# Token sums moved from GpSimd to ScalarE and VectorE, and six weight tiles split once for both token sides, in a decoder trunk on one core

## What is computed

```python
def _adaln(x, gain, mod, j):
    n = _rms(x.astype(jnp.float32)) * gain
    return (n * (1.0 + mod[:, 3 * j + 1]) + mod[:, 3 * j]).astype(x.dtype)

def _swiglu(h, w_gate, w_up, w_down):
    return (jax.nn.silu(h @ w_gate) * (h @ w_up)) @ w_down
```

## Time and profile before

| | us |
|---|---|
| median of three executions | 2867.88 |
| the three | 2866.21, 2867.88, 2873.26 |
| the profiled execution | 2879.42 |
| its span, first to last instruction | 2877.7 |
| TensorE busy in it | 2642.8 (92%) |
| mean granted TensorE clock | 0.942 |

### The profile page before, as it was taken

One profiled execution on the slowest core, in us unless ns is written; L12 is line 12 of the kernel. 1 busy time (PEld: TensorE's weight loads), 2 busy tenths in 40 slices (PEclk: granted clock), 3 DMA queues, 4 the chain that ended last, 5 costly groups with the idle time before them and its releaser, 6 DMA issues. The chain is left out here.

```text
span 2877.7 us, 52261 instructions
## 1 busy us (share of the span) xinstructions
PE 2642.8 (92%) x22580; PEld 2461.4 (86%) x22580; DVE 1719.4 (60%) x2353; ACT 1047.2 (36%) x1484; POOL 775.2 (27%) x530
## 2 busy tenths in 40 slices
PE   3999999999689998899999899999999498899998
PEld 0999988899378876899998899998889378799998
DVE  2868725743466645788852687852632356877824
ACT  2444414322533322444432434442421433444523
POOL 2665201000011021365510156610000121456301
PEclk7999999999689988999999999999999589999999
DMA  6222455721100013332245432255651113322324
GB/s 247 74 89 96 145 182 163 250 85 46 57 2 3 3 55 128 118 103 96 95 169 172 130 103 96 92 173 169 217 187 52 50 20 132 109 92 94 100 81 127
DMA packets 82349, 316.74 MB, mean 110 GB/s; under 512 B 9400, under 2 KB 14408, under 8 KB 80584
## 3 DMA queue, kind: packets, MB, share of 16 engines
q1 hardware_dynamic: 82120, 313.40, 32.7%
HBM read 302.63 MB, written 10.74 MB: 109 GB/s over the span
## 5 line engine op out<-in xcount | busy, mean ns | idle before, releaser
L165 DVE TENSOR_TENSOR weights_r<-work,weights_r 128x1024 fp32r<-128x1024 f32 (+2 forms) x318 | 436.5, 1373 | 356.8 <-ACT weights_r L161 356.5
L161 ACT ACTIVATE weights_r<-work 128x1024 fp32r<-128x1024 f32 (+2 forms) x318 | 313.1, 985 | 584.5 <-PE banks L860 341.8
L756 POOL TENSOR_TENSOR rows<-rows,consts 128x288 f32<-128x288 f32 (+3 forms) x64 | 88.4, 1381 | 691.5 <-ACT consts L967 691.5
L858 PE MATMUL banks<-low_r,weights_r 128*128 128x288 f32 (+2 forms) x1112 | 270.1, 299 | 0.0
L856 PE MATMUL banks<-h_r,weights_r 128*128 128x288 f32 (+1 forms) x904 | 226.0, 305 | 42.0 <-DVE big_r L419 25.8
L858 PE MATMUL banks<-big_r,weights_r 128*128 128x288 f32 (+2 forms) x960 | 244.1, 299 | 0.0
L856 PE MATMUL banks<-low_r,weights_r 128*128 128x288 f32 (+2 forms) x832 | 215.5, 306 | 27.1 <-DVE weights_r L165 18.3
L773 PE MATMUL banks<-h_r,weights_r 128*128 128x288 f32 x788 | 233.1, 296 | 1.6 <-DVE weights_r L165 0.8
L774 PE MATMUL banks<-big_r,weights_r 128*128 128x288 f32 x788 | 232.3, 295 | 0.0
L775 PE MATMUL banks<-h_r,weights_r 128*128 128x288 f32 x788 | 232.1, 295 | 0.0
L860 PE MATMUL banks<-h_r,weights_r 128*128 128x288 f32 (+1 forms) x904 | 221.5, 300 | 0.0
(11 more groups left out here) (550 smaller groups left out, 7079.1 us busy)
## 6 DMA issues: line engine op xcount, KB each, us to landing
work<-w_ff_dram SPq DMA_DIRECT2D x130, 512.0 KB, 3.7
h<-w_mod_dram SPq DMA_DIRECT2D x48, 768.0 KB, 5.3
work<-w_down_dram SPq DMA_DIRECT2D x66, 512.0 KB, 3.5
consts<-w_ff_dram SPq DMA_DIRECT2D x64, 512.0 KB, 3.6
work<-w_mod_dram SPq DMA_DIRECT2D x32, 768.0 KB, 9.1
work<-w_in_even_dram SPq DMA_DIRECT2D x24, 512.0 KB, 3.7
big_buf<-w_mod_dram SPq DMA_DIRECT2D x16, 768.0 KB, 6.0
consts<-w_down_dram SPq DMA_DIRECT2D x22, 512.0 KB, 3.6
```

The costliest lines, as they stand in the source:

```text
L161: return act.activation(high, raw, ACT.Copy)
L165: return engine.tensor_tensor(low, raw, high.bitcast(F32), ALU.subtract)
L756: pool.tensor_tensor(k.rows[:, c], k.rows[:, c], k.square[:, c], ALU.add).then_inc(added, 1)
L858: pe.matmul(out[a], high[:, w], x[a][1], start=False, stop=False)
```

## The change

It has three parts.

1. **Six tiles split once.** In U2 to U4 the side 1 units take the split tiles of side 0 (`add_again`; a `Piece` with `raw` None does nothing on ScalarE and VectorE and has no load). p3, p4 and p5 go to three extra places in `low_r`, which are free once the stage before has ended. p0 to p2 keep the three usual places. So 18 loads, 18 high splits and 18 low splits are gone.
2. **Token sums by VectorE.** L278 is gone: ScalarE adds the shift in place to the scaled tokens that are still there (`shift`, 16 small activations in a stage), and the four sums are made by VectorE (`mix`). GpSimd keeps the weight sums alone.
3. **One more plain unit in U1.** `PLAIN` is 3, so the scheme begins at the fourth unit there. The PSUM pairs of the scheme are rotated by two for it.

```diff
-PLAIN_SKEWED, PLAIN = 4, 2
+PLAIN_SKEWED, PLAIN = 4, 3
...
-    def mix(self, pool, mixed):
-
-
-        norm, n = self.norm, self.sums
-        for a in range(2):
-            pool.wait_ge(norm.low_done[a], KT + a)
-            pool.tensor_tensor(norm.temp[a], norm.high[a].bitcast(F32), norm.low[a].bitcast(F32), ALU.add)\
-                .then_inc(mixed, 1)
...
+    def shift(self, act, a, kt, shifted):
+
+        width = self.norm.prompt[a + 1] - self.norm.prompt[a]
+        at = self.norm.temp[a][:, kt, 0:width]
+        act.activation(at, at, ACT.Identity, bias=self.norm.mod[:, kt, 0:1]).then_inc(shifted, 1)
+
+    def mix(self, dve, name, shifted, mixed):
+        done = self.split + self.order.index(name)
+        if name == "t3":
+            dve.wait_ge(shifted, 2 * KT * (self.number + 1))
+            one, other, op = self.b22, self.b12, ALU.subtract
...
+        dve.tensor_tensor(one, one, other, op).then_inc(mixed, 1)
...
+        def add_again(u, earlier):
+            for i, lo, hi in earlier.pieces:
+                last_use[pieces[i].place] = len(pieces)
+                u.pieces.append((len(pieces), lo, hi))
+                pieces.append(Piece(u, None, None, pieces[i].place, None, pieces[i].nth_split))
...
+            if number:
+                begins = [stage.side_first(a) + 1 + part for a in range(2) for part in range(2)]
+                mixes, highs, lows = (f - 5, f - 4, f - 3, f - 2), (f - 2, f - 2, f - 1, f + 1), (f - 2, f - 1, f - 1, f + 1)
+            else:
+                begins = [f - 6, f - 6, f - 5, f - 5]
+                mixes, highs, lows = (f - 4, f - 3, f - 2, f - 1), (f - 4, f - 3, f - 2, f + 1), (f - 3, f - 2, f - 1, f + 1)
...
                     if stage.kind == "up":
                         if number:
                             pool.wait_ge(piece_done, stage.first)
-                        mixing[stage].mix(pool, tokens_mixed)
...
-                    if i >= SPLIT:
-                        act.wait_ge(piece_done, i - SPLIT + 1)
...
+                    if piece.free_behind >= 0:
+                        act.wait_ge(piece_done, piece.free_behind + 1)
...
+                    for scheme, a, part in shift_at.get(i, ()):
+                        act.wait_ge(scheme.norm.low_done[a], KT + a)
+                        for kt in range(part * KT // 2, (part + 1) * KT // 2):
+                            scheme.shift(act, a, kt, tokens_shifted)
+                    for scheme, name in high_at.get(i, ()):
+                        mixed_high(scheme, name)
```

More of the change, by code:

```diff
@@ L261, in __init__ @@
         self.k, self.stage, self.norm = k, stage, norm
-        self.sums, self.split = 6 * number, 4 * number
+        self.number, self.split = number, 4 * number
+        rotated = 2 * ((PLAIN_SKEWED if norm.after else PLAIN) % 2)
+        self.pairs = [(b + rotated) % 4 for b in range(4)]
         low = lambda t: k.low_r[:, t * T:(t + 2) * T].rearrange("p (k t) -> p k t", k=KT // 2)
@@ L538, in load_of, with add_piece @@
             return loads[-1]
+        last_use, splits, regular = {}, [], [0]
+        places = split + [[k.low_r[:, 10 * T + (2 * i + part) * D:10 * T + (2 * i + part + 1) * D] for part in range(2)]
+                          for i in range(SPLIT)]
+        def add_piece(u, raw_block, ready, lo, hi, extra=None):
+            place = extra
+            if place is None:
+                place = regular[0] % SPLIT
+                regular[0] += 1
+            behind = last_use.get(place, -1)
+            if extra is not None:
+                behind = max(behind, u.stage.units[0].pieces[0][0] - 1)
+            i = len(pieces)
+            splits.append(i)
+            last_use[place] = i
+            u.pieces.append((i, lo, hi))
+            pieces.append(Piece(u, raw_block, ready, place, behind, len(splits)))
+        def add_again(u, earlier):
[3 more added lines that the diff above has]
+                pieces.append(Piece(u, None, None, pieces[i].place, None, pieces[i].nth_split))
         for number, stage in enumerate(stages):
@@ L545, in dense_chain @@
                 stage.units.append(u)
+                again = stage.kind == "up" and sides == (1,)
+                earlier = stage.of.get((m, 0))
                 for a in sides:
@@ L764, in seven_products @@
                     mix, norm = mixing[stage], norms[stage]
-                    bank = lambda pair, side: k.psum_pair(pair)[:, side, 0:HALF]
+                    bank = lambda pair, side: k.psum_pair(mix.pairs[pair])[:, side, 0:HALF]
                     fresh = u is stage.sevens()[0]
                     def product(i, part, tokens, out):
-                        high, low = split[i % SPLIT]
+                        high, low = places[pieces[i].place]
                         for j in range(KT // 2):
@@ L834, in _ @@
                         i, lo, hi = piece
-                        pe.wait_ge(low_done, i + 1)
-                        high, low = split[i % SPLIT]
+                        pe.wait_ge(low_done, pieces[i].nth_split)
+                        high, low = places[pieces[i].place]
                         pair = banks(u, piece)
@@ L1053, in low @@
                 def low(i):
[L1054 to L1057 removed]
+                    piece = pieces[i]
+                    if piece.raw is None:
+                        return
+                    high_part, low_part = (part[:, 0:piece.width] for part in places[piece.place])
+                    dve.wait_ge(high_done, piece.nth_split)
+                    split_low(dve, piece.raw, high_part, low_part).then_inc(low_done, 1)
                 def gate_up(u):
```

129 lines of the change are left out of this document (70 added, 59 removed).

## The result

Timed against the kernel before on the same chip, the changed kernel took 2837.68 us (median of four, 2832.95 to 2840.60), the kernel before 2870.57 us (2866.21 to 2878.98). The ratio is 0.9876, with a 95% interval of 0.9852 to 0.9900, so it is 1.2% faster. (The medians by themselves lie 32.9 us apart, a quotient of 0.9885; the recorded ratio is used throughout.) Timed a second time, beside some of the experiments, it took 2834.29 us, ratio 0.9875 (0.9850 to 0.9900). The forecast was 2831, from 2867.9 - 37.1; from this run's 2870.6 the same sum gives 2833.5, a ratio of 0.9871, inside the interval. The profiled execution took 2840.60 us, 38.8 less than that of before.

A forecast was written before the change was run, and what follows sets the result against it. TensorE, busy 92% of the span, was taken as the bound, with gains from its waits and lower-clock stretches. The terms -4.6, -9.7, -13.0 and -9.8 summed to -37.1 us: from 2867.9 to 2831, range 2819 to 2850.

The forecast's parts named there:

- U1: First stage: first matmul 3.0 us earlier, 3.2 us of waits at the scheme's begin gone, plain unit +1.6; -4.6 us.
- U2: Second stage's head: 8.4 us of waits and 1.7 of lower clock gone, a 0.4 wait at p5 added; -9.7 us.
- U3: Third stage's head: 10.9 us of waits and 4.8 of lower clock gone, 2.7 of waits at p4, p5 added; -13.0 us.
- U4: Fourth stage's head: same pattern as the second stage, with waits of 8.5 us and the same clock loss; -9.8 us.
- B: Rival, heads of U2 to U4: ScalarE's shifts don't hide and delay p4 and p5; +15 us, 2846; chance 0.25.
- C: Rival, scheme's begin: VectorE's token sums collide with GpSimd's weight sums; 6.8 us a stage, 27 in all, 2858; chance 0.06.
- D: Rival, p4 to p11: short waits keep TensorE at 1.2 GHz; 39 us slower, 2907; chance 0.03.
- E: Rival, p6: nothing moves, waits return under other names as side 1's tokens become the bound; 2868; chance 0.04.

The follow-up runs named there:

- e5: The kernel before, with GpSimd's L278 replaced by a memset of the same tile at the same place, its four token sums kept; 2836.48 us in one execution.
- e1: The changed kernel with the scheme begun at the third unit of U1, as before, and that stage's shifts and sums moved up; 2827.79 us, ratio 0.9844.
- e8: The changed kernel with one more GpSimd wait: a unit's first weight sum waits for VectorE's product of the unit two before; 2831.37 us, ratio 0.9862.
- e4: The changed kernel with side 0's eight shifts moved from the iterations of p1 and p2 to those of p5 and p6; 2832.57 us, ratio 0.9857.
- e7: The changed kernel with late side 0 shifts, scheme at U1's third and U2 to U4's fourth unit, t2 split before t1, sums earlier; 2836.82 us, ratio 0.9889.

## Why the prediction was right

**The whole.** Forecast were -37.1 us; the stages gave -39.8, and the timed medians -32.9. The mechanism came as forecast: the waits behind GpSimd's token sums went, and the clock held with them. That the sum of the four terms came so near is in part luck: late waits that the prediction didn't have fell away in U1 (2.4 us) and came up in U2 (2.3 us).

**The cause.** The prediction read from a split of 5.73 us beside L278, from L390 at 2.97 and 3.70 against 0.69, and from the reciprocal's 1.95 beside the same L278 that reading by GpSimd was what held VectorE. e5 shows it: a memset at the same place, of the same size, holds no split. By the rule of the Trainium skill that the prediction named (SBUF — State Buffer, Who interferes with whom) a GpSimd instruction that only writes SBUF doesn't contend with a VectorE instruction of two SBUF inputs; e5 agrees, with 1.23 us beside the memset.

**U1, -4.6 forecast, -8.0 measured.** L394 takes 0.69 us and the first matmul starts at 69.46, against 69.6 forecast: -3.2. In all six places of the changed kernel it is so (shortest, median, longest in ns; first and last start):

```profile
L394 DVE TENSOR_TENSOR big_buf<-work,rows x6: 691/692/693, 65.1 to 2433.4; 128x512 f32<-128x512 f32 x6
```

The waits at the scheme's begin are gone (-3.2), and the plain unit cost 1.2, where I took 1.6 (27.9 + 223.2 us for two plain units and the scheme in e1, 40.3 + 212.0 in the changed kernel). What the term missed is 2.9 us (229.3 us for the scheme of before, less 3.2 of waits, less e1's 223.2): 2.4 late in U1, where the kernel before had the pattern of e8, and 0.5 at the scheme's begin, since a wait costs some 0.25 us more than the idle time that I had counted. Waits of TensorE in the kernel before, 116 to 325:

```profile
PE banks L773 <- DVE weights_r L165: 0.8, 2, 0.4
PE banks L773 <- DVE ring_r L165: 0.4, 1, 0.4
```

I had read the waits of U1 only up to 116 us.

**U2, -9.7 forecast, -8.1 measured.** The head gave 10.4, 0.7 more than the term, as there are three waits fewer and each costs more than its idle time: the wait at p5 is 0.46, forecast 0.4, none is at p4, and the clock is 1.00. Then the scheme lost 2.3, because the same pattern now came up there. This miss and the 2.4 us of U1 are one mechanism, which the prediction didn't have, and they nearly cancel. A slip in the working is small beside it: from the split of p4 to its first matmul give 2.46 us, not 2.3, and the wait at p5 would have been 0.6.

**U3, -13.0 forecast, -12.9 measured.** The waits at p4 and p5 are 1.33 and 1.30, 2.6 together, where I had 1.1 and 1.6, 2.7. The clock, of which I had 4.8 us, is 1.00 over the whole head. e4 shows the first to come from the shifts ahead of the root, as the working had it.

**U4, -9.8 forecast, -10.7 measured.** I had taken its pattern from U2; its wait is 0.49, its head gave 10.4 as U2's did, and its scheme was 0.3 shorter.

**The rivals.** B, that the shifts don't hide, is wrong by its own mark. ScalarE in U2 of the changed kernel:

```profile
1195.29 1.05 ACT L161 ACTIVATE low_r<-consts 128x1024 fp32r<-128x1024 f32 x1
1196.24 1.80 ACT L279 ACTIVATE big_buf<-big_buf,mod 128x288 f32<-128x288 f32 x4
1197.99 0.48 ACT L375 ACTIVATE h_r<-big_buf,mod 128x224 fp32r<-128x224 f32 x1
...
1200.08 1.04 ACT L161 ACTIVATE low_r<-work 128x1024 fp32r<-128x1024 f32 x1
```

The splits of p4 and p5 are 4.79 us apart, as in the earlier trace rows; four shifts fill the idle time and run in 1.80 us, where I took 1.9. C, that the token sums collide with the weight sums, happened and cost nothing. VectorE and GpSimd of the changed kernel at the scheme's begin in U2:

```profile
1226.48 2.31 DVE L165 TENSOR_TENSOR weights_r<-work,weights_r 128x1024 fp32r<-128x1024 f32 x1 [0.50 <-ACT weights_r L161]
1227.79 2.16 POOL L781 TENSOR_TENSOR work<-work 128x512 f32<-128x512 f32 x1
1228.71 2.45 DVE L294 TENSOR_TENSOR big_buf<-big_buf 128x1152 f32<-128x1152 f32 x1
...
1230.03 2.29 POOL L785 TENSOR_TENSOR work<-work 128x512 f32<-128x512 f32 x1
...
1231.09 2.44 DVE L165 TENSOR_TENSOR low_r<-big_buf,low_r 128x1152 fp32r<-128x1152 f32 x1
...
1234.59 2.62 DVE L165 TENSOR_TENSOR low_r<-big_buf,low_r 128x1152 fp32r<-128x1152 f32 x2
```

A sum of 1.35 us becomes 2.45 and two splits of 1.2 and 1.35 become 2.31 and 2.44, some 3.3 us in all. The two splits in the last row end at 1237.2, t2's among them, and t2 is wanted 3.2 us after the scheme's begin at 1237.6, at 1240.8: of the slack 3.6 us is left, where I had 4.5. But t2 is not the tightest, as the working had it. That is t4:

```profile
1243.24 1.93 DVE L165 TENSOR_TENSOR big_r<-big_buf,h_r 128x1152 fp32r<-128x1152 f32 x1
...
1245.56 0.29 PE L816 MATMUL banks<-h_r,ring_r 128*128 128x288 f32 x1
```

Its low part ends at 1245.17 and its first matmul starts at 1245.56, so 0.4 us is left, in U3 and U4 as well. That C cost nothing was a close thing: e8 waits 0.35 us there in U2, and e7, which starts the scheme a unit earlier, 1.2 in each of the three stages. D and E didn't occur: the clock held, and no token of side 1 was late.

**What stays open.** Why the product and the first weight sum come to start in that order in some stages and not in others: the changed kernel and e1 have the same instructions in U2. And what makes the untouched part of the program vary by up to 12 us among profiles of kernels that are alike there.

## What to carry to other kernels

Look at when a GpSimd instruction that reads SBUF runs and which two-input VectorE instructions stand beside it: GpSimd was busy for 27% of the span, and two instructions of it a stage were worth 37 us, because each two-input instruction of VectorE that met one waited to its end. When a change has two parts, ask how much of the gain both would bring alone; here one part had nearly all of it, and a third part cost more than it gave. Read the waits of the whole stage and not of its head alone, since a wait of 0.4 us in every unit is easily overlooked.

## What the runs showed that was not expected

The order of two starts, 0.24 us on one side or 0.35 on the other, decides whether a product of 0.75 us takes 1.84. In the last units of a stage the held order can repeat from unit to unit, five times in U2 of the changed kernel, at 11.85 us a unit (1409.76 to 1421.60, the next one) where it is 11.16 otherwise (1403.11 to 1414.27 in e8); in U3 of the same kernel it turned back by itself after two units, before TensorE had waited. One wait on GpSimd puts it right, and GpSimd's own sum then takes 1.29 us, as alone, in place of 1.46.
